# Deferring the last tile transposes into the next stage, and sharing the state fixup of an SSM scan between VectorE and GpSimd

## The reference, cut to what matters

```python
x = layer_norm(ALPHA * x + 0.5 * swiglu(x, ffn1_w_in, ffn1_w_out), ln1_g, ln1_b)
x = layer_norm(ALPHA * x + token_mixer(x, ...), ln2_g, ln2_b)
x = layer_norm(ALPHA * x + 0.5 * swiglu(x, ffn2_w_in, ffn2_w_out), ln3_g, ln3_b)
e = (p @ ple_w_in) * sigmoid(x @ ple_w_gate)
x = layer_norm(ALPHA * x + e, ln4_g, ln4_b)
# in token_mixer: a gated depthwise convolution over time, and the S5 scan
_, states = lax.associative_scan(combine, (lam_bar, bu), axis=1)   # complex, diagonal
y = einsum("gin,blgn->blgi", c_c, states).real + d_skip * u
```

## Time and profile before

| | |
|---|---|
| device time, median of 3 runs | 2313.05 us (2313.04 to 2318.34) |
| the profiled execution, its own time | 2318.51 us |
| its span on the slowest core (core 2) | 2317.4 us |
| spans of the 8 cores | 2270.0 to 2317.4 us |
| granted TensorE clock, core 2 | 0.828 of full speed |
| PE busy | 1529.3 us (66%) |
| DVE busy | 712.4 us (31%) |
| ACT busy | 553.5 us (24%) |
| POOL busy | 473.5 us (20%) |
| chain that ended last: PE / DMA / DVE | 46% / 14% / 14% |

### The profile page before, as it was taken

How to read it: one execution, slowest core, us unless ns; L and a number is a source line. 1 busy time by engine, 2 the same in 40 slices (tenths; PEclk the granted TensorE clock), 3 DMA queues, 4 the chain that set the end, 5 groups by cost and what they waited for, 6 DMA issues and landing times.

```text
span 2317.4 us, 21611 instructions; the slowest of 8 cores (2270.0 to 2317.4 us)
## 1 busy us (share of the span) xinstructions
PE 1529.3 (66%) x7066; PEld 734.2 (32%) x7200; DVE 712.4 (31%) x1358; ACT 553.5 (24%) x905; POOL 473.5 (20%) x338
## 2 busy tenths in 40 slices
PE   4932168956029847999563799957209957799762
PEld 2410133423024323444222344423105433344320
DVE  1625231214744431212133111213653441111123
ACT  1200112312022331113263111321103241112345
POOL 1100001422003251104234010431002161002424
PEclk7976579978569978999786899978659978899876
DMA  8871353085008039520325952056105309740131
GB/s 130 63 53 6 50 92 46 1 122 53 0 19 76 5 44 164 75 36 1 82 73 120 164 75 33 1 75 85 16 18 49 32 1 160 103 55 1 41 68 46
DMA packets 288174, 135.16 MB, mean 58 GB/s; under 512 B 161344, under 2 KB 267840, under 8 KB 287808
## 3 DMA queue, kind: packets, MB, share of 16 engines
q0 software_dynamic: 180928, 101.72, 34.6%
q1 hardware_dynamic: 107136, 32.04, 7.3%
HBM read 222.87 MB, written 8.39 MB: 100 GB/s over the span
## 4 chain that ended last, share of the span: by engine, by line
PE 46%; DMA 14%; DVE 14%; ACT 8%; SPq 8%; issue 6%; POOL 3%; DVEq 0%; ACTq 0%; POOLq 0%
PE psall L337 44%; DVE arena L347 9%; DMA arena<-ffn_w_in 9%; SPq L141 8%; ACT arena L365 4%; DVE arena L414 3%; DMA arena<-arena 3%; POOL arena L347 2%; ACT L365 2%; DVE arena L356 2%; DMA arena<-ple_w_in 2%; ACT arena L342 2%; DMA arena<-mix_w_in 1%; ACT arena L417 1%; PE psall L401 1%
## 5 line engine op out<-in xcount | busy, mean ns | idle before, releaser
L337 PE MATMUL psall<-arena 128*128 128x512 bf16 (+2 forms) x6362 | 1422.6, 385 | 577.3 <-DMA arena<-arena 224.1
L337 PEld LDWEIGHTS psall<-arena 128*128 128x128 bf16 (+1 forms) x6496 | 640.2, 102 | 1347.9 <-issue 665.7
L347 POOL TENSOR_TENSOR arena<-arena 128x1024 f32<-128x1024 f32 x128 | 300.1, 2345 | 688.7 <-ACT arena L365 678.8
L365 ACT ACTIVATE arena<-psall 128x512 f32<-128x512 f32 (+1 forms) x320 | 189.1, 597 | 706.2 <-PE psall L337 690.0
L347 DVE TENSOR_TENSOR arena<-arena 128x16 f32<-128x16 f32 (+7 forms) x568 | 271.6, 478 | 165.4 <-DMA arena<-conv_b 58.5
L347 DVE TENSOR_TENSOR arena<-arena,psall 128x512 bf16<-128x512 f32 x176 | 120.9, 688 | 518.7 <-PE psall L337 466.6
L143 POOL DMA_DIRECT2D arena<-ffn_w_in x88 | 77.6, 892 | 597.8 <-PE psall L337 477.5
L347 DVE TENSOR_TENSOR arena<-psall,arena 128x512 f32<-128x512 f32 (+1 forms) x136 | 89.8, 688 | 329.2 <-PE psall L337 136.3
L401 PE MATMUL psall<-arena 128*128 128x128 f32 x512 | 87.7, 332 | 144.2 <-POOL arena L347 98.9
L365 ACT ACTIVATE arena<-arena 128x1 f32<-128x1 f32 (+2 forms) x268 | 140.9, 526 | 83.4 <-DVE arena L356 35.4
L417 ACT ACTIVATE arena<-arena 128x1024 bf16<-128x1024 f32 x64 | 67.6, 1056 | 325.9 <-DVE arena L414 325.9
(11 more groups left out here) (37 smaller groups left out, 133.4 us busy)
## 6 DMA issues: line engine op xcount, KB each, us to landing
arena<-ffn_w_in POOLq DMA_DIRECT2D x88, 512.0 KB, 12.7
arena<-ffn_w_out POOLq DMA_DIRECT2D x8, 1536.0 KB, 29.0
arena<-ffn_w_out POOLq DMA_DIRECT2D x8, 1280.0 KB, 42.7
arena<-x SPq DMA_DIRECT2D x16, 512.0 KB, 5.7
arena<-mix_w_in POOLq DMA_DIRECT2D x32, 256.0 KB, 5.1
out<-arena SPq DMA_DIRECT2D x16, 512.0 KB, 2.6
arena<-arena SPq DMA_DIRECT2D x16, 256.0 KB, 3.2
arena<-ln_g SPq DMA_DIRECT2D x8, 512.0 KB, 5.5
```

The lines of the kernel that those rows point to most:

```text
L337: kb.op("pe", lambda e: e.matmul(out, lhsT=lhsT, rhs=rhs, start=start, stop=stop), reads, writes, mark)
L347: kb.op(en, lambda e: e.tensor_tensor(out, a, b, op), reads, writes, mark)
L365: kb.op("act", lambda e: e.activation(out=out, in_=in_, func=func, **kw), reads, writes, mark)
```

## The change

Two independent edits. First, the transposes at a stage's end are put on a list, and `flush_pending()` issues them in the next stage: in `ffn` and `mixer` after the first group of 16 matmuls with its ACT and DVE step, in `ple` after the matmuls, sigmoids and multiplies of tile 3, ahead of its layer norm. Second, the 8 fixup operations of the scan are issued as two sets, groups 0 to 7 on DVE and groups 8 to 15 on POOL, each of 8 operations of 128x1024, with buffers of their own.

```diff
+    pending_tr = []
+    def flush_pending():
+        while pending_tr:
+            transposes_tile(pending_tr.pop(0))
 ...
 # ffn, after each group's silu and multiply
+                    flush_pending()
 # ffn, end
-        transposes_tile(7)
+        pending_tr.append(7)
 # mixer, after each group's copy and multiply of the first loop
+                flush_pending()
 # mixer, the fixup
-        tt("dve", TF1, pwr, cbr, ALU.mult, *RW)
-        tt("dve", TF2, pwi, cbi, ALU.mult, *RW)
-        tt("dve", TF1, TF1, TF2, ALU.subtract, *RW)
-        tt("dve", sre, sre, TF1, ALU.add, *RW)
-        tt("dve", TF1, pwr, cbi, ALU.mult, *RW)
-        tt("dve", TF2, pwi, cbr, ALU.mult, *RW)
-        tt("dve", TF1, TF1, TF2, ALU.add, *RW)
-        tt("dve", sim, sim, TF1, ALU.add, *RW)
+        for hh, en_ in ((0, "dve"), (1, "pool")):
+            gsl = slice(8 * hh, 8 * hh + 8)
+            TF1 = view(R1o + 8 * KBY * hh, F32, [8, 8, 16])
+            TF2 = view(R1o + 8 * KBY * hh + 4 * KBY, F32, [8, 8, 16])
...
+            tt(en_, TF1, pwr, cbr, ALU.mult, Rr, Ww)
+            tt(en_, TF2, pwi, cbi, ALU.mult, Rr, Ww)
+            tt(en_, TF1, TF1, TF2, ALU.subtract, Rr, Ww)
+            tt(en_, sre, sre, TF1, ALU.add, Rr, Ww)
+            tt(en_, TF1, pwr, cbi, ALU.mult, Rr, Ww)
+            tt(en_, TF2, pwi, cbr, ALU.mult, Rr, Ww)
+            tt(en_, TF1, TF1, TF2, ALU.add, Rr, Ww)
+            tt(en_, sim, sim, TF1, ALU.add, Rr, Ww)
-        copy_op("act", SBF, SS[:, :, :, 0:128], [bS], [bSBF])
+        copy_op("act", SBF, SS[:, :, :, 0:128], [bS, bS2], [bSBF])
 # mixer, end
-        transposes_tile(6)
-        transposes_tile(7)
+        pending_tr.append(6)
+        pending_tr.append(7)
 # ple, before ln(s)
+            if s == 3:
+                flush_pending()
```

More of the change, by code:

```diff
@@ L848, in mixer @@
             tt("dve", cur, T1s, lend, ALU.add, [bS], [bSBF])
[L849 to L855, removed]
@@ L856, in mixer @@
-        sim = SS[:, :, 1, 1:129].rearrange("p g (b k) -> p g b k", b=8)
-        RW = ([bE, bS, bSBF, bSM], [bE, bS])
-        tt("dve", TF1, pwr, cbr, ALU.mult, *RW)
-        tt("dve", TF2, pwi, cbi, ALU.mult, *RW)
-        tt("dve", TF1, TF1, TF2, ALU.subtract, *RW)
-        tt("dve", sre, sre, TF1, ALU.add, *RW)
-        tt("dve", TF1, pwr, cbi, ALU.mult, *RW)
-        tt("dve", TF2, pwi, cbr, ALU.mult, *RW)
-        tt("dve", TF1, TF1, TF2, ALU.add, *RW)
-        tt("dve", sim, sim, TF1, ALU.add, *RW)
+        bFX = [Buf(), Buf()]
@@ new lines, in mixer @@
+        bS2 = Buf()
+        kb.handoff([bE], bFX)
+        kb.handoff([bS], [bS2])
+        for hh, en_ in ((0, "dve"), (1, "pool")):
+            gsl = slice(8 * hh, 8 * hh + 8)
+            TF1 = view(R1o + 8 * KBY * hh, F32, [8, 8, 16])
+            TF2 = view(R1o + 8 * KBY * hh + 4 * KBY, F32, [8, 8, 16])
+            pwr = PW16[:, 0, gsl, :].unsqueeze(2).broadcast_to([128, 8, 8, 16])
+            pwi = PW16[:, 1, gsl, :].unsqueeze(2).broadcast_to([128, 8, 8, 16])
+            cbr = CB[:, gsl, 0, 0:8].unsqueeze(3).broadcast_to([128, 8, 8, 16])
+            cbi = CB[:, gsl, 1, 0:8].unsqueeze(3).broadcast_to([128, 8, 8, 16])
+            sre = SS[:, gsl, 0, 1:129].rearrange("p g (b k) -> p g b k", b=8)
+            sim = SS[:, gsl, 1, 1:129].rearrange("p g (b k) -> p g b k", b=8)
+            bSh = bS if hh == 0 else bS2
+            Rr, Ww = [bFX[hh], bSh, bSBF, bSM], [bFX[hh], bSh]
+            tt(en_, TF1, pwr, cbr, ALU.mult, Rr, Ww)
[6 more added lines that the diff above has]
+            tt(en_, sim, sim, TF1, ALU.add, Rr, Ww)
@@ L866, in mixer @@
         copy_op("dve", SC, CB[:, :, :, 8], [bSBF], [bSC])
-        copy_op("act", SBF, SS[:, :, :, 0:128], [bS], [bSBF])
+        copy_op("act", SBF, SS[:, :, :, 0:128], [bS, bS2], [bSBF])
         bSSTK = Buf()
-        kb.handoff([bE], [bSSTK])
+        kb.handoff([bE] + bFX, [bSSTK])
         for par in range(2):
@@ L895, in mixer @@
         kb.handoff([bSSTK], [bMG])
-        kb.handoff([bS], bMT)
+        kb.handoff([bS, bS2], bMT)
         for ft in range(8):
@@ L946, in mixer @@
                 transposes_tile(s - 2)
-        transposes_tile(6)
-        transposes_tile(7)
-        return ([bSU, bE, bSSTK, bMG, bV, bS, bCBZ] + bMT,
+        pending_tr.append(6)
+        pending_tr.append(7)
+        return ([bSU, bE, bSSTK, bMG, bV, bS, bS2, bCBZ] + bMT + bFX,
                 [bUT, bSBF, bZ, bSTM, bSTT, bWMO])
```

## The result

| | before | after |
|---|---|---|
| median | 2318.46 us (10 runs) | 2356.56 us (9 runs) |
| ratio of the comparable runs | | 1.0151, 95% interval 1.012 to 1.0181 |
| profiled execution, slowest core | 2317.4 us (core 2) | 2355.5 us (core 3) |

The change makes the kernel slower by 1.5%: +38 us by the medians, +35 us by the ratio, which leaves disturbed executions out. The forecast was +38 on the median of before as it was then, 2313, at 2351 us.

What follows compares the result with a forecast made beforehand. No engine bounds the kernel; PE waits in one chain at stage boundaries and in the scan. Fixup 19, bundles 14, mixer's start 4.6 and ple 0.4 sum to +38 us, 2351 us on the median; range 2328 to 2366.

Steps and rivals of the forecast that it cites:

- The fixup: Scan: DVE and POOL exclude each other, 28.6 us against 19.1, +9.5 a half, +19 in all.
- my allowance of a quarter more: Fixup: POOL may read operands that repeat elements a quarter slower, +5 a half at most.
- The bundles: After the scan: weight loads delayed behind POOL's fixup share DMA engines with four SSTK DMAs, +7 a half, +14 in all.
- The bound of +10.7: SSTK DMAs: upper bound from a prologue DMA stretched from 3.2 to 10.25 us by overlapping weight loads.
- estimate of 6.4 us: SSTK DMAs: with equal turns between queues a 3.2 us transfer takes about 6.4, +7 to +10 over two or three.
- the count of bytes: SSTK DMAs and bundles: 2.7 MB and 1 MB at 178 GB/s end together at T+22, +5 a half.
- Mixer's start: First ffn to mixer: transposes and DVE's copy follow the first 16 matmuls, +2.3 a half, +4.6 in all.
- Second ffn: Mixer to second ffn: +3.1 us for PE, hidden by the wait for the fourth slot's weights, cost 0.
- ple: Second ffn to ple: copies fit into existing waits in tile 3; 0 to 0.7 a half, +0.4 taken in all.
- No exclusion: Rival, fixup: DVE and POOL run in parallel on these operands, +0.8 a half, +21 in all, 2334 us; chance 0.1.
- SP's DMAs pass the bundles: Rival, after the scan: the small SSTK DMAs pass the weight loads, +24 in all, 2337 us; chance 0.15.
- The deferral pays: Rival, stage boundaries: matmuls fill the norm wait if weights are there, up to 6.1 us each, about 2313; chance 0.06.

Runs made afterwards that it cites:

- defer_only: The deferred transposes alone, fixup all on DVE, against the kernel before: ratio 1.0013 (0.9984 to 1.0043).
- defer_not_mixer: Transposes deferred only into the second ffn and ple, fixup all on DVE, against the kernel before: ratio 0.9991 (0.9953 to 1.0029).
- split_in_turn: The shared fixup alone, with POOL's set waiting for DVE's whole set, against the kernel before: one run, 2356.56 us (before 2308.9).
- split_psum: Shared fixup, first three weight bundles issued ahead, DVE's set replaced by multiplies with second input in PSUM: one run, 2293.9 us (before 2308.1).
- split_bundles_first: The shared fixup alone, with the first three weight bundles issued ahead of POOL's operations, against the kernel before: ratio 1.0045 (1.0009 to 1.0081).
- split_only: The shared fixup alone, transposes back at the stages' ends, against the kernel before: ratio 1.0167 (1.0127 to 1.0208).

## Why the prediction was right, by its steps

- **The fixup, +9.5 a half predicted, +5.4 measured.** Mechanism right, size off. The term 8 x (1.23 + 2.34) used POOL's row on plain operands; with the fixup's repeated operands POOL takes 2.09, less and not more, so my allowance of a quarter more went the wrong way (2.0 of the 4.1 us), and 0.3 us of each pair overlaps (2.2). 8 x 3.04 = 24.3 us. The forecast rows, DVE's at 3.5 and POOL's at 2.35, had only DVE waiting; each waits for the other, and the rows are 2.71 and 2.91.
- **The bundles, +7 a half predicted, +10.0 measured.** Mechanism right, size off. The bound of +10.7 from the row of the prologue comes near the sum, but not by its parts: two DMAs are stretched, to 7.4 and 8.1 us, and not one to 10.25, which was besides the longest of that DMA on the eight cores (8.5 to 10.3). The prediction's estimate of 6.4 us for a DMA at half speed, +7 to +10 in all, fits the parts better than either; the count of bytes, towards which I leaned, fits least.
- That the total came out so near is in part luck: the two errors, 4.1 too much and 3.0 too little, nearly cancel, 16.5 a half predicted and 15.4 measured.
- **Mixer's start, +2.3 predicted, 2.4 in the profiled core, +3.0 by the stretch.** The row by row account holds. By the medians the distance from the mixer's first matmul is 2.4 longer at the second group's ACT step and still 2.4 at PE's next long wait, the 15 us for DVE ahead of the last projection; behind that it grows to 3.0 in `defer_only` and 2.6 in after. Why is not shown.
- **Second ffn, 0 predicted.** Shown by the fourth slot's shorter wait with the same end (55.0 and 54.2 us) and by `defer_not_mixer`. **ple, 0.2 a half predicted**: the copy stands inside the sum's wait, as said, and the eighth sum ends 89.1 us into the stage in both.
- **The rivals.** No exclusion: refuted by `split_in_turn` (without it the fixup would have been 1.0 a half shorter and not 0.8 longer, by `split_psum`). SP's DMAs pass the bundles: refuted by 11.04 us and by `split_bundles_first`. The deferral pays: its condition was right, its price was not. Put at up to 6.1 us a boundary, it is 2 us at one boundary of a half and nothing that I can see at the others, even with the weights there.
- The sum, 2 x (8.0 + 10.0) = 36 us, lies between the two measures of the whole, 35 and 38. The low end of the range, 2328, doesn't come out of its terms: the lower rival's 2334 less 0.6 for the cheaper transposes is 2333. Nothing hangs on it.

## What to carry to other kernels

Before work is moved to another engine, ask what stands behind it in that engine's queue: here POOL's eight operations cost less by their length than by the weight loads that they pushed into the path of a small DMA. Sharing elementwise work between DVE and POOL gave nothing here, at either share, while DVE read both inputs from SBUF, and would have given 1 us of 19 with one of them in PSUM. And filling a wait is worth nothing if it isn't the last of the waits at that place: find what the engine waits for last (here loads that stood in a queue behind a layer norm) and move that, which gave 3.7% with no change to the work.

## What the runs showed that I had not expected

- POOL's two-input operations of 1024 float32 elements take 2.34 us on plain operands but 1.93 to 2.34, on average 2.09, in the fixup. Alone in `split_in_turn`, the four multiplies whose operands repeat elements take 1.93, the two operations on plain temporaries 2.34, and the two that add into the states 2.16.
- Of four DMAs of 256 KB, issued one after the other beside the bundles, the first two took 7.4 and 8.1 us by the medians instead of 3.2 and 3.0, less than half the speed. In single cores either went up to 11 to 13 us: in core 6 of `split_only` PE started 34.1 us after the cast, against 26.2 in core 2 of the same execution. Since the slowest core sets the time, such cores cost more than the medians say.
